# Modulation vectors of a ten-stage transformer: row products on VectorE and row sums on ScalarE in place of column products and partition sums on TensorE

## The reference

```
cond = silu(c)                                       # c: (1, 1024)
for i in range(2):
    mod = (cond @ w_mod[i] + b_mod[i]).reshape(-1, 3, 3, 1024)   # w_mod[i]: (1024, 9216)
    h = rms_norm(x, g) * (1 + mod[:, 0, 1]) + mod[:, 0, 0]
    x = x + 0.5 * mod[:, 0, 2] * swiglu(h)
    h = rms_norm(x, g) * (1 + mod[:, 1, 1]) + mod[:, 1, 0]
    x = x + mod[:, 1, 2] * mixer(h)                  # i = 0: bidirectional SSD, i = 1: latent attention
    h = rms_norm(x, g) * (1 + mod[:, 2, 1]) + mod[:, 2, 0]
    x = x + 0.5 * mod[:, 2, 2] * swiglu(h)
```

## Time and profile before

| what | value |
|---|---|
| median of 3 runs | 2430.26 us (2426.51 to 2432.41) |
| the profiled execution | 2425.49 us, span 2423.7 us |
| TensorE matmul busy | 2128.3 us (88%) |
| VectorE busy | 1620.8 us (67%) |
| ScalarE busy | 992.0 us (41%) |
| DMA | 379.33 MB, mean 157 GB/s |
| in the chain of waits | PE 72%, DVE 20%, ACT 4%, issue 3%, DMA 2% |
| modulation on VectorE: L828 | 343 instructions, 211.4 us, 616 ns each |
| modulation on TensorE: L987 | 147 matmuls in two passes, 294 instructions |

### The profile page before, as it was taken

How to read it: one execution, slowest core, us unless ns; L and a number is a source line. 1 busy time by engine, 2 the same in 40 slices (tenths; PEclk the granted TensorE clock), 3 DMA queues, 4 the chain that set the end, 5 groups by cost and what they waited for, 6 DMA issues and landing times.

```text
span 2423.7 us, 35322 instructions
## 1 busy us (share of the span) xinstructions
PE 2128.3 (88%) x14424; PEld 1908.3 (79%) x14424; DVE 1620.8 (67%) x2579; ACT 992.0 (41%) x1572; POOL 0.2 (0%) x4
## 2 busy tenths in 40 slices
PE   7729679999888899999999878489999999768998
PEld 7619569999865699999999855369999999456998
DVE  4467479884155698878857879658787753276555
ACT  4321054454144554443345633244334332345332
POOL 0000000000000000000000000000000000000000
PEclk9769589999877899999989999789998998878999
DMA  7200038746220487667644310047766652303551
GB/s 295 93 0 1 1 136 298 279 140 226 94 98 1 152 286 275 234 234 276 254 148 158 139 53 1 0 165 262 282 225 245 237 183 90 132 1 108 199 188 70
DMA packets 114849, 379.33 MB, mean 157 GB/s; under 512 B 4993, under 2 KB 5121, under 8 KB 113921
## 3 DMA queue, kind: packets, MB, share of 16 engines
q1 hardware_dynamic: 114688, 377.08, 43.3%
HBM read 376.01 MB, written 1.05 MB: 156 GB/s over the span
## 4 chain that ended last, share of the span: by engine, by line
PE 72%; DVE 20%; ACT 4%; issue 3%; DMA 2%; DVEq 0%; SPq 0%; ACTq 0%
PE psum L873 29%; PE psum L889 14%; PE psum L651 7%; PE psum L704 4%; DVE htok L1854 2%; DVE buf L569 2%; PE psum L645 2%; PE psum L1130 2%; PE psum L1483 1%; PE psum L2272 1%; DMA ring<-in_w_ffn 1%; PE psum L1727 1%; PE psum L856 1%; DVE buf L2053 1%; PE psum L498 1%
## 5 line engine op out<-in xcount | busy, mean ns | idle before, releaser
L873 PEld LDWEIGHTS psum<-buf,buf 128*128 128x128 f32 x6048 | 741.5, 192 | 12.9 <-DVE buf L787 4.0
L873 PE MATMUL psum<-buf,buf 128*128 128x256 f32 x6048 | 746.2, 283 | 2.0 <-DVE buf L787 2.0
L889 PE MATMUL psum<-buf,buf 128*128 128x512 f32 x1584 | 384.1, 391 | 3.3 <-DVE buf L936 3.3
L889 PEld LDWEIGHTS psum<-buf,buf 128*128 128x128 f32 x1584 | 289.1, 188 | 59.7 <-DVE buf L936 5.0
L787 DVE TENSOR_TENSOR buf<-ring,buf 128x2048 fp32r<-128x2048 f32 x132 | 301.9, 2287 | 43.3 <-ACT buf L781 42.4
L651 PE MATMUL psum<-buf,buf 128*128 128x256 f32 x2064 | 255.0, 284 | 9.5 <-DVE buf L569 9.4
L651 PEld LDWEIGHTS psum<-buf,buf 128*128 128x128 f32 x2064 | 249.2, 192 | 15.0 <-DVE buf L569 15.0
L781 ACT ACTIVATE buf<-ring 128x2048 fp32r<-128x2048 f32 x132 | 251.3, 1904 | 20.3 <-DMA ring<-in_w_ffn 20.3
L803 DVE TENSOR_TENSOR buf<-ring,buf 128x1024 fp32r<-128x1024 f32 x132 | 161.5, 1223 | 144.4 <-ACT buf L798 144.1
L569 DVE TENSOR_TENSOR buf<-ring,buf 128x1024 fp32r<-128x1024 f32 x132 | 161.3, 1224 | 118.0 <-ACT buf L563 108.7
L798 ACT ACTIVATE buf<-ring 128x1024 fp32r<-128x1024 f32 x132 | 139.3, 1055 | 191.6 <-PE psum L889 189.1
(11 more groups left out here) (318 smaller groups left out, 2362.0 us busy)
## 6 DMA issues: line engine op xcount, KB each, us to landing
ring<-in_w_ffn SPq DMA_DIRECT2D x88, 1536.0 KB, 6.5
modw<-in_w_mod SPq DMA_DIRECT2D x98, 768.0 KB, 6.9
ring<-in_w_conv SPq DMA_DIRECT2D x44, 1536.0 KB, 6.5
ring<-in_w_ssd_in SPq DMA_DIRECT2D x16, 1536.0 KB, 6.6
ring<-in_w_ns_in SPq DMA_DIRECT2D x9, 1536.0 KB, 7.6
ring<-in_w_hy_in SPq DMA_DIRECT2D x7, 1536.0 KB, 19.2
ring<-in_w_ssd_out SPq DMA_DIRECT2D x5, 1536.0 KB, 6.5
ring<-in_w_cmp SPq DMA_DIRECT2D x4, 1024.0 KB, 4.7
```

What stands on the lines that cost most here:

```text
L873: ins = E.matmul(b[:, g * T:(g + 1) * T], w[:, wa, g, k, :], h[:, ha, k, :], start=k + n_ == 0, stop=k == KC - 1 and n_ == 2)
L889: ins = E.matmul(acc[:, t, g * 512:(g + 1) * 512], hr[z][:, ha, t * P:(t + 1) * P], wd[z][:, wa, g * 512:(g + 1) * 512], start=j == 0 and ...
```

## The change

The modulation weights are laid out transposed: a group is now 128 output rows (partitions) by 1024 inputs. silu(c) lies as a row of 1024, the same on each partition (`crow`). For each group VectorE multiplies weights by `crow`, in place in one of three `modw` slots (`mod_products`), and ScalarE copies the product onto itself with its accumulator on, which leaves the row's sum in `modT` (`mod_sums`). The even iterations have two groups, the odd ones one. `macc`, `add_up` and its 33 matmuls per stage are gone; the bias is added on VectorE. The modulation loads are issued behind `hidden` and the sums; at a stage change both first ones stand behind `weights(1)`. silu(c) is computed on 128x1024, its input comes by one more DMA of 0.5 MB. To make room in the memory, the ssd stage keeps its C matrix in `modw`, and moves some buffers.

```diff
     }
-    arrays["w_mod"] = np.concatenate([col_chunks(w) for w in i["w_mod_2"]], 0)
+    arrays["w_mod"] = np.concatenate([np.asarray(w).T for w in i["w_mod_2"]], 0).reshape(-1, P, D)
     for l in range(2):
...
         "rows": np.stack([np.broadcast_to(i[name][l], (P, D)) for l in range(2) for name in ("mix_post_g", "ffn_post_g")]),
+        "c_row": np.broadcast_to(i["c_2"][0], (P, D)),
         "x": np.ascontiguousarray(i["x"][0].reshape(NT, P, D).transpose(1, 0, 2)).reshape(P, NT * D),
...
         modw = sb("modw", SLOT)
+        crow = sb("crow", D)
         posi = sb("posi", NT, I32)
...
             row_free = go
-            mods = [0, 0]
-            mod_free = [go, go]
-            mod_last = go
-            macc_free = go
-            sums_taken = go
+            mods = 0
+            mod_free = [go] * 3
...
                                                         scale=1.0 / D).then_inc(act.sem, 1)))
-
-            if sums is not None:
-                sums["add_up"]()
...
-        def ffn(name, gain, shift, conv=None, row=None, gate=None, pieces=range(0)):
+        def ffn(name, gain, shift, conv=None, row=None, gate=None, mods=range(0)):
...
-            slot, up_split, down_split, up, down, mult, hid, mod_in = {}, {}, {}, {}, {}, {}, {}, {}
+            slot, up_split, down_split, up, down, mult, hid, mod_in, mod_prod = {}, {}, {}, {}, {}, {}, {}, {}, {}
...
-            def mod_weights(i):
-                piece, half = todo[i]
-                free = Ring.mod_free[half]
-                Ring.mods[half] += 1
-                mod_in[i] = (mod_full[half], 16 * Ring.mods[half])
-
-                @block.sync
-                def _(sp):
-                    sp.wait_ge(*free)
-                    sp.dma_start(modw[:, half * 1536:(half + 1) * 1536].rearrange("p (c w) -> p c w", c=3),
-                                 dram["w_mod"][3 * piece:3 * piece + 3].rearrange("c p w -> p c w")
-                                 [:, :, half * 512:(half + 1) * 512]).then_inc(mod_full[half], 16)
+            def mod_weights(j):
+                for c in due[j]:
+                    z = Ring.mods % 3
+                    free = Ring.mod_free[z]
+                    Ring.mods += 1
+                    mod_in[c] = z, (mod_full[z], 16 * ((Ring.mods + 2) // 3))
+
+                    @block.sync
+                    def _(sp):
+                        sp.wait_ge(*free)
+                        sp.dma_start(modw[:, z * D:(z + 1) * D], dram["w_mod"][c]).then_inc(mod_full[z], 16)
...
-            def mod_ops(i, ks):
-
-                if not 0 <= i < len(todo):
-                    return
-                piece, half = todo[i]
-                w = modw[:, half * 1536:(half + 1) * 1536].rearrange("p (c k n) -> p c k n", c=3, k=KC // 2)
-                m = piece - pieces[0]
-                o = macc[:, m * 3 * P:(m + 1) * 3 * P].rearrange("p (c n) -> p c n", c=3)
-
-                @block.vector
-                def _(_e):
-                    for k in ks:
-                        kc = half * (KC // 2) + k
-                        if k == 0:
-                            V.wait_ge(*mod_in[i])
-                        if kc == 0:
-                            if m == 0:
-                                V.wait_ge(*Ring.macc_free)
-                            ins = V.tensor_scalar(o, w[:, :, 0, :], cond[:, 0:1], None, ALU.mult)
-                        else:
-                            V.wait_ge(*Ring.mod_last)
-                            ins = V.scalar_tensor_tensor(o, w[:, :, k, :], cond[:, kc:kc + 1], o, ALU.mult, ALU.add)
-                        Ring.mod_last = dve.count(ins.then_inc(dve.sem, 1))
-                        if k == KC // 2 - 1:
-                            Ring.mod_free[half] = Ring.mod_last
+            def mod_products(j):
+
+                for c in due[j]:
+                    z, full = mod_in[c]
+                    w = modw[:, z * D:(z + 1) * D]
+
+                    @block.vector
+                    def _(_e):
+                        V.wait_ge(*full)
+                        mod_prod[c] = dve.count(V.tensor_tensor(w, w, crow[:, :], ALU.mult).then_inc(dve.sem, 1))
+
+            def mod_sums(j):
+
+                for c in due[j]:
+                    z = mod_in[c][0]
+                    w = modw[:, z * D:(z + 1) * D]
+
+                    @block.scalar
+                    def _(_e):
+                        A.wait_ge(*mod_prod[c])
+                        Ring.mod_free[z] = act.count(A.activation(w, w, ACT.Copy, accum_out=modT[:, c:c + 1]).then_inc(act.sem, 1))
...
                 weights(0)
-                for i in range(min(2, len(todo))):
-                    mod_weights(i)
                 if gate is not None:
...
                 weights(1)
+                mod_weights(0)
+                mod_weights(1)
                 split_up(1, free)
...
                                                                       cv[z], ALU.mult, ALU.add).then_inc(dve.sem, 1))
-                        mod_ops(step, (tap - 1,))
...
                     row_point = gate_row(mod_col(*gate, 2), 0.5, 0, [h_pts[-1]])
-                mod_ops(0, range(KC // 2))
+                mod_products(0)
                 for j in range(1, NF):
...
                         weights(j + 3)
-                    if 2 <= j + 1 < len(todo):
-                        mod_weights(j + 1)
                     if j >= 2:
...
                     pe_up(j)
-                    hidden(j - 1, j)
+                    hidden(j - 1)
+                    mod_sums(j - 1)
+                    mod_weights(j + 1)
                     pe_down(j - 1, row_point)
                     split_down(j, [down[j - 2, 1]] if j >= 2 else [h_pts[-1]])
-                    mod_ops(j, range(2 if c3 else 0, KC // 2))
+                    mod_products(j)
                 if nxt is not None:
                     nxt["pre_a"]([up[NF - 2]])
-                hidden(NF - 1, NF)
+                hidden(NF - 1)
+                mod_sums(NF - 1)
                 if nxt is not None:
...
-                def add_up():
-                    last = (dve.sem, Ring.mod_last[1])
-
-                    @block.tensor
-                    def _(_e):
-
-                        E.wait_ge(*last)
-                        for c in range(3 * len(pieces)):
-                            ins = E.matmul(bank(7)[:, c:c + 1], macc[:, c * P:(c + 1) * P], one_col, start=True, stop=True)
-                        Ring.macc_free = pe.count(ins.then_inc(pe.sem, 1))
-
-                def finish():
-                    a = 3 * pieces[0]
-                    n = 3 * len(pieces)
+                def bias():
+                    a, n = mods[0], len(mods)
...
                     def _(_e):
-                        V.wait_ge(*Ring.macc_free)
-                        Ring.sums_taken = vl(V.tensor_tensor(modT[:, a:a + n], bank(7)[:, 0:n],
-                                                             prm("b_mod")[:, a:a + n], ALU.add).then_inc(dve.sem, 1))
-                sums = dict(add_up=add_up, finish=finish) if len(pieces) else None
+                        V.wait_ge(*mods_done)
+                        vl(V.tensor_tensor(modT[:, a:a + n], modT[:, a:a + n], prm("b_mod")[:, a:a + n], ALU.add).then_inc(dve.sem, 1))
+                mods_done = Ring.mod_free[(Ring.mods - 1) % 3]
                 add = add_normed if gate is None else add_gated
-                return add([down[NF - 1, 0], down[NF - 1, 1]], row_point), sums
+                return add([down[NF - 1, 0], down[NF - 1, 1]], row_point), (bias if len(mods) else None)
...
                 A.activation(wa[0:64, :], wa[0:64, :], ACT.Tanh)
-                A.activation(cond, prm("c"), ACT.Sigmoid)
+                A.wait_ge(crow_in, 16)
+                A.activation(rowc, crow[:, :], ACT.Sigmoid)
                 Ring.p = act.count(A.activation(glo, glo, ACT.Sigmoid).then_inc(act.sem, 1))
...
                     V.wait_ge(*point)
-                V.tensor_tensor(cond, cond, prm("c"), ALU.mult)
+                V.tensor_tensor(crow[:, :], crow[:, :], rowc, ALU.mult)
                 vl(V.tensor_scalar(ld_, ld_, -math.exp(-0.5), None, ALU.mult).then_inc(dve.sem, 1))
+                Ring.mod_free = [(dve.sem, dve.n)] * 3
                 for c in range(4):
...
             ar = Region(W_AT + 24576)
-            bc = ar.take(16 * T).rearrange("p (c t) -> p c t", t=T)
+            bT = ar.take(8 * T).rearrange("p (c t) -> p c t", t=T)
+            cT = modw[:, 0:8 * T].rearrange("p (c t) -> p c t", t=T)
+            ar.at = R_AT
             zs_ = ar.take(16 * T)
...
             y_done = [(dve.sem, dve.n), (pe.sem, pe.n)]
+            Ring.mod_free = [y_done[1]] * 3
...
                                                              inv[:, (c // 2) * T:(c // 2 + 1) * T], ALU.mult, ALU.mult).then_inc(dve.sem, 1))
-            done = out_project("w_ssd_out", 16, xb, [(dve.sem, dve.n), (act.sem, act.n), (pe.sem, pe.n)], nxt, H_AT)
```

(19 more changed lines are left out.)

33 lines of the change are left out of this document (17 added, 16 removed).

## The result

| | before | after |
|---|---|---|
| median of 5 runs, same chip | 2426.51 us (2425.22 to 2432.41) | 2438.82 us (2435.56 to 2441.53) |
| ratio | | 1.0047, 95% interval 1.0035 to 1.0059 |
| profiled execution (span) | 2425.49 (2423.7) | 2440.38 (2438.6) |

The change makes the kernel 12 us slower, and 14.9 us between the two profiled executions. A second series of 12 runs, beside later experiments, gave 1.0037 (1.0022 to 1.0052).

A forecast was written before the change was run, and what follows sets the result against it. TensorE bounds the conv loops before, a VectorE-ScalarE ring after. Terms 11.0 + 11.6 - 6.5 - 5.4 + 0 + 1.7 + 2.0 = +14.4 us on the median 2430.26 gave 2444.7 us, range 2432 to 2454.

The forecast's parts named there:

- The ring: Conv stages: VectorE and ScalarE's in-order loop takes 9.12 and 9.03 us against TensorE's 8.50, costing 14.5 us per stage.
- The price of a sum: ScalarE row sum on 128x1024 inside the conv loops: 1.05 us each, bounds 0.95 and 1.15.
- Tails of the conv stages: From the conv loops' last steps to the next stage's first block: +11.0 and +11.6 us, loop loss included.
- Ends of ffn00 and ffn01: Next blocks come earlier without add_up at ffn00, -6.5 us, and without the late load at ffn01, -5.4 us.
- The clock term: First block behind an idle TensorE runs slower: 0.7 us added at ffn00's end, 0.8 at ffn01's.
- Starts of the gated stages: Two sums stand before the second down-weight copy in three gated stages: +0.57 us each, together +1.7, bounds 0 and 3.
- Hybrid: Hybrid stage: sigmoid and product on 1024 columns instead of 8, on the path: +2.0 us, bounds 1.5 and 2.2.
- the load at the start: Extra 0.5 MB load at the kernel's start: taken as 0, or 1 to 2 us if not covered.
- ssd: The ssd stage: 0 us change expected.
- doesn't bind: Rival: conv loops stay at TensorE's 8.50 us, 14.5 us less in all, 2415.8 us; chance 0.10.
- Half binds: Rival: ScalarE and VectorE overlap more, conv loop 8.8 us instead of 9.08, 2434 us; chance 0.12.
- the clock gives way: Rival: TensorE's waits slow its conv blocks, iteration 9.3 us, +9.5 us, 2454 us; chance 0.08.

The follow-up runs named there:

- Experiment 1: The changed kernel with the row sums moved ahead, right behind ScalarE's copy of the up weights, next loads issued with them: 2409.92 us, ratio 0.9921.
- experiment 2: The changed kernel with each row sum of the two conv stages done twice on ScalarE: 2516.75 us, ratio 1.0362.
- Experiments 3 to 5: Kernel before with first two modulation loads behind weights(1): 2415.77 us, again 2415.69; with add_up cut to one matmul: 2417.48; with both: 2406.16.
- experiment 6: silu(c) off the path in the change: 2428.18 us; same with sums moved ahead: 2407.50; change repeated: 2435.93; kernel before with wide silu(c): 2431.25.

## Why the prediction was right, step by step

The measured time lies in the range, and the mechanism that decides it is the predicted one.

- **The ring** (the step that decides): right in mechanism and size. Predicted 9.12 and 9.03 us, measured 9.09 and 8.99. From L798(0) to L782(21) 182.0 us were measured (360.07 to 542.05) and 182.7 predicted. Experiment 1 takes it away and experiment 2 stretches it, both by what the addition says. In the timeline above each term stands from start to start: 2.20, 1.03, 0.32, 1.05, 1.07, 1.14, twice 1.14.
- **The price of a sum**: 1.05 us at 128x1024, taken from the spacing of the 128x256 ones; measured 1.04 to 1.05 (373.82 to 374.87). The read of the accumulator (0.18 to 0.19 us in the timeline) lies under the next copy.
- **Tails of the conv stages**: +9.85 for +11.0 and +10.7 for +11.6. L432 came at 558.46 - 7.9 = 550.6 for 551.4, of which 0.7 is the shorter ring. The other part is the slower first block: I added 0.7 in conv0, it was 0.5 (6.32 for 5.84); in conv1 I added nothing, and it was -0.2 (6.49 for 6.66). In conv1 ScalarE's wait of 4.24 us for the weights is gone, as predicted.
- **Ends of ffn00 and ffn01**: -7.0 for -5.9 and -5.9 for -4.8, with the starts of the gated stages counted in. Experiments 3 to 5 show the parts: add_up at ffn00, both load and add_up at ffn01, where neither alone gives the whole. The clock term of these ends (0.7 and 0.8) was not there at ffn00 (5.87 us for 5.94).
- **Starts of the gated stages**: predicted +0.57 us each. In ffn00, from the first of the two sums to L782 are 5.33 us (below) for the 4.90 of the earlier trace rows, +0.43.

```profile
1074.88 2.07 ACT modw L822 x4
...
1080.21 2.29 DVE buf L782
```

- **Hybrid**: predicted +2.0 with bounds 1.5 and 2.2. Silu(c)'s own part was 1.9, so the term was right; the load at the start, put at 0, cannot be told (the change is 0.2 to 0.7 us behind there, and traces with before's code lie 0.7 us before to 0.6 us behind it). What went wrong is that I took the rest of an unchanged stage as fixed: it ended at +7.9, and the stage's length differs by 5 us between two executions of one kernel, with TensorE's clock (experiment 6).
- **ssd**: predicted 0, measured -2.85 between first blocks (391.45 us for 394.3), which leaves add_up out. Of this, too, one can't say that the change did it: the six traces with the ssd code of before have 391.95 to 396.4 us.
- **The rivals**: "doesn't bind" priced the version without the ring at 14.5 us under before; experiment 1 is 17 to 19 under. "Half binds" and "the clock gives way" are out: the ring is 9.04 us, and its waits left the up blocks at 6.0 us, first start to last end, where they were 5.9 before; the granted clock over the loop was 0.99.

The median fell 5.9 us below the prediction, 3.8 of them because this chip ran the kernel before at 2426.5 and not at 2430.3, and inside the range. Part of the agreement is luck: without the 4.5 us of clock in the hybrid stage the profiled execution would have been some 10 us over before, still in the range but nearer to its lower end. The same holds for the other sign, as ssd's -2.85 was not foreseen either.

## What to carry to other kernels

Busy shares do not price a move of work between engines. Where two in-order engines hand work to each other in each iteration, add up the circle from start to start, and compare it with the period of the engine that sets the pace; here work put into the circle counted whole, on an engine that had a third of its time free, and the same work a few instructions earlier, beside the longest step of the other engine, counted nothing. Two things that end at nearly the same time at a stage's end must be removed together, and be priced together.

## What was not expected of the hardware

- One kernel's hybrid stage took 339.6 or 344.7 us, 3.8 us of the difference in 64 matmuls that took 5.98 us at a granted clock of 1.00 and 9.74 at 0.58. A difference of 5 us there between two single profiles says nothing of an edit. The nsa stage, whose code is the same in all 13 profiles, took 275.0 to 284.2 us between first blocks.
- The one-column fp32 matmuls follow the clock as well: a pass every 112 ns at 1.00 and every 213 ns at 0.50. Though TensorE ran them back to back, the clock fell from its upper level to its lower one in the middle of them, behind conv0 in the kernel before after 21 of 66.
- 24 such passes in TensorE's idle time ahead of a stage left the next block at 6.40 us against 6.38.
